# Stick-breaking attention: the later key tiles are summed on VectorE before the minus-ones product

## What is computed

```python
def stick_breaking_attention(q, k, v):
    for i in range(s // BLOCK_Q):                 # BLOCK_Q = 128
        z = jnp.einsum('bhqd,bhkd->bhqk', qh[:, :, st:ln], kh[:, :, :ln]) * scale
        past = np.arange(ln)[None, :] < np.arange(st, ln)[:, None]
        l = jnp.where(past, jax.nn.log_sigmoid(-z), 0.0)
        a = jnp.where(past, jnp.exp(z + reverse_cumsum_keys(l)), 0.0)
        outs.append(jnp.einsum('bhqk,bhkd->bhqd', a, vh[:, :, :ln]))
```

## Time and profile before

| what | value |
|---|---|
| median of three runs | 3435.17 us (3432.92 to 3439.03) |
| the profiled execution | 3427.3 us |
| its span | 3425.5 us |
| TensorE busy | 3097.4 us, 90% |
| VectorE busy | 1119.8 us, 33% |
| ScalarE busy | 645.4 us, 19% |
| mean granted clock of TensorE | 0.945 |

### The profile page before, as it was taken

One profiled execution on the slowest core, in us unless ns is written; L12 is line 12 of the kernel. 1 busy time (PEld: TensorE's weight loads), 2 busy tenths in 40 slices (PEclk: granted clock), 3 DMA queues, 4 the chain that ended last, 5 costly groups with the idle time before them and its releaser, 6 DMA issues.

```text
span 3425.5 us, 31538 instructions
## 1 busy us (share of the span) xinstructions
PE 3097.4 (90%) x12171; PEld 1674.4 (49%) x12171; DVE 1119.8 (33%) x1865; ACT 645.4 (19%) x1148; POOL 193.4 (6%) x234
## 2 busy tenths in 40 slices
PE   4999675688959999978999999999989999999998
PEld 3444345444447877853455444444434554444444
DVE  3355475675741111122331223331023312233300
ACT  2232412100021111113232111110032311111100
POOL 1000011310001111121000000000000000000000
PEclk7999887898969999989999999999999999999999
DMA  6200000575728999972211212222112012222220
GB/s 218 73 26 25 0 1 1 198 288 203 290 88 305 353 355 338 359 248 88 74 50 49 74 49 74 81 89 70 65 44 94 30 49 74 74 74 74 74 72 39
DMA packets 232992, 413.51 MB, mean 121 GB/s; under 512 B 8337, under 2 KB 137917, under 8 KB 232749
## 3 DMA queue, kind: packets, MB, share of 16 engines
q1 hardware_dynamic: 204800, 314.59, 26.7%
q0 software_dynamic: 27552, 96.17, 7.7%
q10 hardware_dynamic: 525, 1.19, 0.1%
HBM read 386.73 MB, written 25.19 MB: 120 GB/s over the span
## 4 chain that ended last, share of the span: by engine, by line
PE 82%; DMA 7%; DVE 4%; issue 4%; ACT 2%; POOL 0%; SPq 0%; ACTq 0%; POOLq 0%; DVEq 0%
PE PSALL L435 50%; PE PSALL L2221 9%; PE PSALL L1547 6%; DMA AR<-idx_rows 3%; PE PSALL L1555 3%; DMA AR<-hn_rows,AR 2%; DMA W<-in_w_branch_b 1%; PE PSALL L405 1%; PE PSALL L1807 1%; PE PSALL L1102 1%; PE PSALL L711 1%; PE PSALL L730 1%; DVE TMP L414 1%; PE PSALL L335 1%; PE PSALL L449 1%
## 5 line engine op out<-in xcount | busy, mean ns | idle before, releaser
L435 PE MATMUL PSALL<-HN,W 128*128 128x512 f32 x2848 | 1271.7, 603 | 45.0 <-DMA W<-in_w_branch_b 28.2
L435 PEld LDWEIGHTS PSALL<-HN,W 128*128 128x128 f32 x2848 | 541.3, 193 | 729.7 <-issue 693.1
L435 PE MATMUL PSALL<-AR,W 128*128 128x512 f32 x752 | 331.8, 598 | 9.0 <-issue 4.5
L2221 PE MATMUL PSALL<-AR,W 128*128 128x512 f32 x704 | 302.5, 592 | 0.0
L1547 PE MATMUL PSALL<-AR,W 128*128 128x128 f32 x2560 | 291.6, 276 | 7.2 <-DVE AR L1588 7.0
L1547 PEld LDWEIGHTS PSALL<-AR,W 128*128 128x128 f32 x2560 | 288.6, 193 | 10.4 <-issue 10.4
L435 PEld LDWEIGHTS PSALL<-AR,W 128*128 128x128 f32 x752 | 142.7, 191 | 187.5 <-issue 181.0
L2221 PEld LDWEIGHTS PSALL<-AR,W 128*128 128x128 f32 x704 | 133.8, 190 | 168.4 <-issue 168.4
L2199 DVE TENSOR_SCALAR AR<-AR,VEC 128x512 f32<-128x512 f32 x88 | 42.9, 488 | 390.2 <-ACT AR L2179 390.2
L526 DVE TENSOR_TENSOR H<-H,TMP 128x512 f32<-128x512 f32 x40 | 27.7, 692 | 411.2 <-ACT TMP L511 411.2
L2179 ACT ACTIVATE AR<-PSALL 128x512 f32<-128x512 f32 x88 | 52.6, 598 | 533.4 <-PE PSALL L435 533.4
(11 more groups left out here) (447 smaller groups left out, 2696.4 us busy)
## 6 DMA issues: line engine op xcount, KB each, us to landing
W<-in_w_up SPq DMA_DIRECT2D x84, 1024.0 KB
W<-in_w_in SPq DMA_DIRECT2D x26, 2048.0 KB
AR<-in_w_ada POOLq DMA_DIRECT2D x24, 2048.0 KB, 8.2
W<-in_w_gate SPq DMA_DIRECT2D x40, 1024.0 KB
W<-in_w_down SPq DMA_DIRECT2D x40, 1024.0 KB
y_rows<-AR SPq DMA_DIRECT2D x40, 512.0 KB, 10.7
AR<-in_ada_w POOLq DMA_DIRECT2D x8, 2048.0 KB, 8.8
W<-in_w_down SPq DMA_DIRECT2D x8, 2048.0 KB
```

Source lines behind the costliest of these rows:

```text
L435: mm = pe.matmul(o, l, r, start=(i == 0), stop=(i == len(products) - 1))
L2221: mm = pe.matmul(PS[g % 4][:, :], w[:, k - k0, m * P:(m + 1) * P], FF[:, k, :], start=(k == 0), stop=(k == FT - 1))
```

## The change

In `sums`, the loop over the later key tiles is replaced by a loop over what a new function `later(h, j)` gives. VectorE adds later tiles up in a buffer `TAIL[h % 2]` of 3 x 128 columns, in a part of the arena that no tile uses at that time: columns 0 to 127 hold tile 2 plus tile 3 on the queries of tile 3; columns 128 to 255 hold tile 1 plus tile 2 on the queries of tile 2; columns 256 to 383 hold tiles 1, 2 and 3 on the queries of tile 3. The additions stand in `softplus`, one behind tile 2 and two behind tile 1, each behind a wait on tiles already finished. The products with minus ones for tile 0 are then 128 and 256 columns wide (before 384, 256, 128), for tile 1 128 and 128 (before 256, 128), and for tile 2 128, as before.

```diff
-DVE_LAYER = 189
+DVE_LAYER = 193
@@ sums
-                    for i in range(j + 1, NT):
-                        add(mask["negones"], past(sp, i), i * P, False)
+                    for tile, o in later(h, j):
+                        add(mask["negones"], tile, o, False)
@@
+        TAIL = [ar(13312 + 3 * P * x, 3 * P) for x in range(2)]
+
+        def later(h, j):
+
+            sp, tail = SPB[h % 2], TAIL[h % 2]
+            return [[(past(sp, 1, P, 2 * P), P), (tail[:, P:3 * P], 2 * P)], [(past(sp, 2, 2 * P, 3 * P), 2 * P), (tail[:, 0:P], 3 * P)],
+                    [(past(sp, 3), 3 * P)], []][j]
@@ softplus
+                    tail, cols = TAIL[h % 2], lambda i, c: past(SPB[h % 2], i, c * P, (c + 1) * P)
+                    if j == 2:
+                        dve.wait_ge(sb_sp, L * 16 + (4 * h + 1))
+                        own(dve.tensor_tensor(tail[:, 0:P], cols(2, 3), cols(3, 3), ALU.add))
+                    elif j == 1:
+                        dve.wait_ge(sb_sp, L * 16 + (4 * h + 2))
+                        dve.tensor_tensor(tail[:, P:2 * P], cols(1, 2), cols(2, 2), ALU.add)
+                        dve.tensor_tensor(tail[:, 2 * P:3 * P], cols(1, 3), tail[:, 0:P], ALU.add)
```

## The result

Twenty runs of each kernel gave a median of 3421.11 us for the changed kernel (3409.65 to 3429.89) and 3430.68 us for the kernel before (3420.37 to 3439.03); the three runs known ahead of the prediction are among the latter. The ratio is 0.9973, with a 95% interval of 0.9962 to 0.9983: about 9.3 us less, between 5.8 and 13.0. The forecast gain of 6.9 us (ratio 0.9980) lies inside that interval; the forecast time of 3428.3 us, and its range from 3423 to 3434, lie above the measured median.

The account below looks back on a forecast made before the run. TensorE, busy throughout the stage, was taken as the bound. Fewer columns save 8 x 0.86 = 6.9 us, VectorE's additions were costed at zero, so 3435.17 - 6.9 = 3428.3 us, range 3423 to 3434.

Parts of the forecast that it names:

- The bound and the columns: In the sums, TensorE never pauses; 512 of 3072 columns fewer per head save 0.86 us, 6.9 us in all.
- The slack to the weighing: Weighing of head 0 needs ScalarE's last exponential, which would be ready with 3.6 us slack, so no gain is lost.
- The additions: Three VectorE additions per head in the softplus loop take 0.74 us (0.63 to 0.96), costed at zero because covered.
- the cover: 16 gate products before each pair's sums, 13.73 us, hide the additions; without them each first pair pays up to 1.5 us.
- (c): Sums: a product costs by being a product, not by columns; 0.37 us per head, 3.0 us gained, 3432.2 us; chance 0.03.
- (d): Additions before head 1's last tile: VectorE becomes late, kernel slower; 3443 us if one addition costs 2 us; chance 0.04.
- (b): Behind the sums: granted clock after later stalls shifts; two drops more or fewer give 3431.7 or 3424.9 us; chance 0.13.
- The level: Whole kernel: base time 3435.17 us, median of three timed runs, with about 2 us each side for the spread.
- The chances: Whole kernel against a 0.2% line, 6.87 us: faster 0.45, same 0.52, slower 0.03.

Follow-up runs that it names:

- the twelve further additions: Changed kernel with 12 more VectorE additions per head behind tile 2, each waited for, written where nothing reads them; 3435.02 us in a single execution.
- The uncovered kernels: Kernel before and changed kernel, each with the 16 gate products moved behind each pair's sums; one run each, 3467.78 us (before) and 3470.32 us (changed).
- the cut product: Changed kernel with tile 0's product over 256 columns cut into two of 128; 3422.32 us in a single execution.
- the additions alone: Kernel before plus VectorE's three additions per head, their results unused and TensorE's products the old ones; ratio 1.0013 (0.9997 to 1.0028).
- the change with the mask: Changed kernel with the diagonal mask added to scores in PSUM by VectorE, replacing TensorE's identity product; 3418.45 us against 3432.50 for the kernel before, ratio 0.9964.
- the two repeats: Changed kernel unedited, again beside the kernel before: 3424.72 us against 3432.60, ratio 0.9983, and 3424.25 against 3433.07, ratio 0.9979.
- the kernels with the mask on VectorE: VectorE adds the mask in PSUM instead of TensorE's identity product: on the changed kernel 3418.45 us, on the kernel before 3428.60 us.

## Why the prediction was right in the gain and wrong in the time

**The bound and the columns: right.** TensorE was the bound of the stage, and is. A head was to lose 0.86 us and lost 0.85 (1.71 us per pair, 6.8 in all); 52 records and 8.7 us per pair were named, 8.75 came; the stage was to be 69.3 to 69.4 us and is 69.4. From the stage's start to the end, three profiles of the changed kernel give 1698.2, 1698.3 and 1698.3 us against 1704.8 in the one of the kernel before: 6.5 to 6.7 us. The slack to the weighing, the DMAs and the norms behind the stage took nothing back.

**The additions: right in the sum, two terms of the working off.** I priced the one that is waited for at 0.32 us and it is 0.41. The difference goes with the wait for ScalarE's semaphore that stands behind it: of the twelve further additions each stands 0.33 us ahead of the next, and the last, behind which the same wait stands, 0.40. So a head costs VectorE 0.81 us and not 0.74; still within the bounds of 0.63 and 0.96. And the cover was put down to the 16 gate products alone, with up to 1.5 us to pay without them. The uncovered kernels show TensorE waiting for the first tile only. For the 1.5 us I had compared VectorE's end with TensorE's start. But each tile has its own wait, and the sums of one tile cover the making of the next. That is shown with sums that begin at the 1.2 GHz level; at 2.4 GHz it is reckoned, with 0.1 us to spare.

**The rivals.** (c) is refuted by the cut product. The rule of the Trainium skill that stood beside it ("TensorE: Matmul & The Clock Gate", section "Back-to-back issue gap") does not hold for this float32 stream: the product of 512 columns takes 1.52 - 0.44 - 0.22 = 0.86 us in tile 0 after the change, four times the 0.22 us of 128 columns and not 1.6 times. (d) exists as a mechanism, at four to five times the added work. (b) did not show: in the stretch between the stages of the two layers the granted clock is 0.99 and the length is 855.61 us before and 855.78 after, and behind the second stage it is 703.60 and 703.50 us.

**The level: wrong, and this put the time outside the range.** The step that failed is the level: "I keep the difference, not the level: 3435.17 - 6.9", the median of three runs, with only "about 2 us on each side for the spread of the runs" around it. Over twenty runs the same kernel has 3430.68 us, 4.5 us less, and single runs lie between 3420.37 and 3439.03. The three were high ones: the other seventeen have 3429.63. The rows to see it were there: the profiled execution stood 7.9 us below the median, outside the spread of the three runs, so a single execution moves by more than that. With the level of twenty runs the forecast would have been 3430.68 - 6.9 = 3423.8, and the same working would have given a range from about 3418 to 3429, in which 3421.11 lies. The remaining 2.7 us are within the interval of the comparison.

Where the level comes from is seen in the runs' own columns. Each run lists its span and its mean granted clock. Over the changed kernel's twenty runs the spans scatter with a standard deviation of 5.7 us, and the product of span and clock with 2.1 us; span and clock are correlated at -0.92. So most of the scatter goes with the clock that TensorE was granted; that one sets the other is not shown. By the profiles it arises ahead of the stage: that stretch was 1709.1, 1724.5 and 1728.9 us long in three profiles of the changed kernel and 1720.7 in the one of the kernel before, while the rest repeats to 0.2 us for one kernel. What decides how much clock is granted there was not tried.

The product can also be taken as a measure of the gain. Its means are 3229.6, 3230.0 and 3232.3 for the changed kernel (20, 12 and 8 runs) and 3237.5, 3238.0 and 3237.4 for the kernel before (29, 17 and 18 runs): weighted by runs 7.3 us between them, with a standard error of about 0.6. That fits the 6.9 us. But it is a rougher measure than its standard error says: for the additions alone it gives 2.1 us less (12 runs), where the stretch is 0.4 us longer, and for the change with the mask 16.9 us (12 against 17 runs), where the stretch gives 13.7. So a further part of a microsecond or two, ahead of the stage, can't be excluded.

**The chances.** I gave 0.45 to faster by over 0.2%, since the sum lay on that line. The first comparison put it at 0.27% (0.17 to 0.38), the two repeats at 0.17% and 0.21%: on the line, as reckoned. On which side of the line a comparison then falls is largely luck.

## What to carry to other kernels

Where TensorE is busy all of a stage and another engine idles, count the columns that TensorE streams with a constant matrix (ones, identity): sums over tiles and masks can be made by the idle engine first, and each column taken away was worth its full time here, as long as that engine is not late. To see whether the other engine is in time, compare tile by tile, each result with the moment at which its own wait stands, and not the end of the one engine with the start of the other. A forecast of a gain and one of a time are two forecasts; for the time, take the level and its spread from many runs, and judge small gains by the stretch from the change to the end in the profile.

## What was not expected of the hardware

- VectorE can add onto scores in PSUM between two products that accumulate there: the later products went on from its values (the kernels with the mask on VectorE). Such a 128x128 addition has a start-to-start time of some 0.23 us (8 in 1.81 us).
- After 9.0 us without work TensorE took 1.44 us for a tile of sums that takes 0.66 us otherwise, at a granted clock of 0.50 and not 1.00. On top of the waits this costs 2.3 to 2.7 us per pair of sums in the uncovered kernel before (12.72 and 13.12 against 10.46) and 2.5 to 3.1 us in the uncovered changed one (11.22 to 11.88 against 8.75). After the 2.3 us of wait in the kernel with more additions the granted clock stayed at 1.00.
- The same instructions ahead of the stage took from 1709.1 to 1728.9 us in three profiles of one program, more than the whole change is worth.
